# Grouped-query attention of a four-layer block on one Trainium2 core: heads one by one, or in pairs

## What is computed

```python
# third layer (mixer_a): band of radius 128 and a sink per head
s = einsum('bnqhgd,bnkhd->bnhgqk', qb, kw) * HEAD_DIM ** -0.5
s = where(mask, s, -inf)
m = maximum(max(s, -1), sink)
p = exp(s - m);  denom = sum(p, -1) + exp(sink - m)
o = einsum(p, vw) / denom
# fourth layer (mixer_b) and all memory heads: softmax(q k^T * HEAD_DIM ** -0.5) v, no mask, no sink
# (mixer_b: q and k pass an RMS norm with a gain per head first)
x = x + rms_norm(concatenate([tok, mo]) @ w_o[i], g_mix_post[i])
```

## Time and profile before

| | |
|---|---|
| median, lowest, highest of 3 | 1790.45, 1789.71, 1795.37 us |
| profiled execution | 1794.06 us, span 1792.3 us |
| PE busy (matmuls) | 1694.7 us, 95% |
| DVE busy (VectorE) | 1246.4 us, 70% |
| ACT busy (ScalarE) | 964.7 us, 54% |
| mean granted clock of TensorE | 0.976 |
| heads of the third layer, first scores to first tile of the projection | 1194.25 to 1234.79 us |
| heads of the fourth layer, the same | 1515.16 to 1553.18 us |

### The profile page before, as it was taken

One profiled execution on the slowest core, in us unless ns is written; L12 is line 12 of the kernel. 1 busy time (PEld: TensorE's weight loads), 2 busy tenths in 40 slices (PEclk: granted clock), 3 DMA queues, 4 the chain that ended last, 5 costly groups with the idle time before them and its releaser, 6 DMA issues.

```text
span 1792.3 us, 29338 instructions
## 1 busy us (share of the span) xinstructions
PE 1694.7 (95%) x10696; PEld 1502.6 (84%) x10696; DVE 1246.4 (70%) x1826; ACT 964.7 (54%) x1580; POOL 74.9 (4%) x74
## 2 busy tenths in 40 slices
PE   7999999799999999998899999988899978989997
PEld 6999987499999899986689999866799977689996
DVE  6876785357666786676757776767776677667665
ACT  5655563455554655555545654556555554755453
POOL 0100110000000100011201000000000002000000
PEclk9999999899999999999999999999899988989998
DMA  6665454145655465554234656531365534036552
GB/s 226 208 210 185 157 173 152 48 165 192 204 178 188 138 219 194 180 181 132 83 133 150 207 191 193 178 122 51 107 215 191 185 119 141 32 110 215 191 190 73
DMA packets 79331, 287.04 MB, mean 160 GB/s; under 512 B 8848, under 2 KB 9232, under 8 KB 79008
## 3 DMA queue, kind: packets, MB, share of 16 engines
q1 hardware_dynamic: 78336, 282.25, 47.8%
q0 software_dynamic: 608, 3.15, 0.5%
q10 hardware_dynamic: 320, 0.74, 0.1%
HBM read 285.05 MB, written 1.05 MB: 160 GB/s over the span
## 4 chain that ended last, share of the span: by engine, by line
PE 35%; issue 11%; DVE 6%; ACT 3%; DMA 1%; POOL 0%; POOLq 0%; SPq 0%; ACTq 0%; DVEq 0%
PE ps L1805 8%; PE ps L1746 5%; PE ps L1809 4%; PE ps L1791 4%; PE ps L1793 4%; PE ps L1792 4%; PE ps L2131 2%; PE ps L2095 1%; DMA raw<-units 1%; DVE inv L1601 1%; ACT prob L1033 1%; PE ps L1679 1%; DVE wlo L1090 1%; PE ps L2119 1%; DVE x L1323 1%
## 5 line engine op out<-in xcount | busy, mean ns | idle before, releaser
L1254 DVE TENSOR_TENSOR wlo<-raw,whi 128x1024 fp32r<-128x1024 f32 x380 | 463.4, 1223 | 128.1 <-ACT whi L850 126.8
L1805 PE MATMUL ps<-acts,whi 128*128 128x512 f32 x2016 | 506.9, 393 | 1.5 <-DVE prob L1261 0.9
L850 ACT ACTIVATE whi<-raw 128x1024 fp32r<-128x1024 f32 x380 | 398.1, 1051 | 100.1 <-PE ps L1809 70.1
L1805 PEld LDWEIGHTS ps<-acts,whi 128*128 128x128 f32 x2016 | 362.9, 189 | 67.5 <-DVE prob L1261 1.3
L1791 PE MATMUL ps<-hid_hi,wlo 128*128 128x256 f32 x1056 | 298.8, 283 | 0.0
L1792 PE MATMUL ps<-hid_hi,whi 128*128 128x256 f32 x1056 | 298.8, 283 | 0.0
L1793 PE MATMUL ps<-hid_lo,whi 128*128 128x256 f32 x1056 | 298.8, 283 | 0.0
L1809 PEld LDWEIGHTS ps<-acts,wlo 128*128 128x128 f32 x2016 | 275.0, 190 | 19.7
L1809 PE MATMUL ps<-acts,wlo 128*128 128x256 f32 x2016 | 281.1, 282 | 0.0
L1090 DVE TENSOR_TENSOR wlo<-raw,whi 128x1024 fp32r<-128x1024 f32 x154 | 187.4, 1236 | 131.1 <-ACT whi L724 130.5
L724 ACT ACTIVATE whi<-raw 128x1024 fp32r<-128x1024 f32 x154 | 159.6, 1054 | 140.3 <-DMA raw<-units 103.0
(11 more groups left out here) (194 smaller groups left out, 1898.6 us busy)
## 6 DMA issues: line engine op xcount, KB each, us to landing
raw<-units SPq DMA_DIRECT2D x534, 512.0 KB, 4.0
arena<-mem_in POOLq DMA_DIRECT2D x2, 1024.0 KB, 7.1
x<-x_in SPq DMA_DIRECT2D x4, 256.0 KB, 4.7
arena<-mem_in POOLq DMA_DIRECT2D x4, 256.0 KB, 4.9
out<-x SPq DMA_DIRECT2D x4, 256.0 KB, 2.1
const<-const_in ACTq DMA_DIRECT2D x1, 560.0 KB, 5.1
row<-row_in ACTq DMA_DIRECT2D x1, 134.0 KB, 5.7
gain<-gain_in SPq DMA_DIRECT2D x1, 76.5 KB, 1.9
```

Of the source, the lines that this page charges most:

```text
L850: nc.scalar.activation(whi[:, u % RING, :], raw[:, u % RAW, :], ACT.Copy).then_inc(hi_ready, 1)
L1254: V.tensor_tensor(wlo[:, u % RING, :], raw[:, u % RAW, :], whi[:, u % RING, :].bitcast(F32), ALU.subtract).then_inc(lo_ready, 1)
L1805: T.matmul(ps[:, bank, :], whi[:, slot, w], acts[:, k].rearrange("p e s -> p (e s)"), start=k == 0, stop=False)
```

## The change

Both grouped-query layers call a new loop, `pair_attention`, with eight pairs instead of sixteen heads; the linear and the latent layer keep `attention`. The pairs have semaphores of their own. VectorE adds the mask, takes the maximum, scales, adds the sink's share, takes the reciprocal and multiplies once for two heads (the scaled maximum is made in place in `top`). ScalarE copies both heads' transposed probabilities in one instruction from banks 4 and 5, so that `probT` is filled once a pair. TensorE puts the outputs of both heads in one bank, head 0 on partitions 0 to 63 and head 1 on 64 to 127, with the matmuls of the two heads in alternation. VectorE, and no longer ScalarE, writes the high part; it covers both heads with one copy and then one subtraction. The steps also shift: scores of pair `s`, transposes of pair `s`-2 and outputs of pair `s`-3 on TensorE; maximum of `s`, multiplication of `s`-2 and split of `s`-4 on VectorE; exponentials of `s`-1 and copy of `s`-3 on ScalarE.

The core of the diff (new semaphores, `self.done` and the calls of `pair_attention` left out; a semaphore wait that names `base + p + 1` waits for pair `p`):

```diff
# helpers
+        def pair_scores(p):
+            return ps[:, 2 * (p % 2):2 * (p % 2) + 2, :].rearrange("p e (t k) -> p e t k", t=TT)
+        def of_pair(a, p):
+            return a[:, 2 * (p % 2):2 * (p % 2) + 2]
# ScalarE, for s in range(n + 4), n = 8
+                        if 1 <= s <= n:
+                            p = s - 1
+                            act.wait_ge(pair_top, base + p + 1)
+                            if p >= 2:
+                                act.wait_ge(pair_turned, base + p - 1)
+                            for e in range(2):
+                                job, j = jobs[2 * p + e], 2 * (p % 2) + e
...
+                            ins.then_inc(pair_exp, 1)
+                        if 3 <= s < n + 3:
+                            p = s - 3
+                            act.wait_ge(pair_turned, base + p + 1)
+                            if p >= 1:
+                                act.wait_ge(pair_out, base + p)
+                            nc.scalar.activation(probT[:].rearrange("p e k q -> p (e k q)"),
+                                                 ps[:, 4:6, :].rearrange("p e n -> p (e n)"), ACT.Copy
+                                                 ).then_inc(pair_copied, 1)
+                        if s >= n + 4 - AHEAD:
+                            self.split(1)
# VectorE, for s in range(n + 4)
+                        if s < n:
+                            p, job = s, jobs[2 * s]
+                            dve.wait_ge(pair_scored, base + p + 1)
+                            if job["mask"] is not None:
+                                middle = of_pair(ps, p)[:, :, P:3 * P]
+                                self.step(V.tensor_tensor(middle, middle, job["mask"].unsqueeze(1).to_broadcast([P, 2, 2 * P]),
+                                                          ALU.add))
+                            self.step(V.tensor_reduce(of_pair(top, p), pair_scores(p), AX_X, ALU.max))
...
+                            ins.then_inc(pair_top, 1)
+                        if 2 <= s < n + 2:
+                            p, job = s - 2, jobs[2 * s - 4]
+                            dve.wait_ge(pair_exp, base + p + 1)
...
+                            self.step(V.reciprocal(of_pair(inv, p), of_pair(total, p)))
+                            V.tensor_tensor(of_pair(prob, p), of_pair(prob, p),
+                                            of_pair(inv, p).unsqueeze(3).to_broadcast([P, 2, TT, S]), ALU.mult
+                                            ).then_inc(pair_prob, 1)
+                        if s >= n + 4 - AHEAD:
+                            self.split(1)
+                        if s >= 4:
+                            p, kt = s - 4, jobs[2 * s - 8]["kt"]
+                            dve.wait_ge(pair_out, base + p + 1)
+                            o = ps[:, 6 + p % 2, 0:S]
+                            V.tensor_copy(act_hi[:, kt, :], o).then_inc(pair_hi, 1)
+                            dve.wait_ge(pair_hi, base + p + 1)
+                            V.tensor_tensor(act_lo[:, kt, :], o, act_hi[:, kt, :].bitcast(F32), ALU.subtract
+                                            ).then_inc(pair_lo, 1)
# TensorE, for s in range(n + 3)
+                        if s < n:
+                            if s >= 2:
+                                pe.wait_ge(pair_exp, base + s - 1)
+                            for t in range(TT):
+                                for e in range(2):
+                                    job = jobs[2 * s + e]
+                                    ins = T.matmul(pair_scores(s)[:, e, t, :], job["q"][t], job["k"], start=True, stop=True)
+                            ins.then_inc(pair_scored, 1)
+                        if s == n:
+                            pe.wait_ge(pair_exp, base + n)
+                            self.out_tile(0)
+                        if s == n + 1:
+                            self.out_tile(1)
+                        if 2 <= s < n + 2:
+                            p = s - 2
+                            pe.wait_ge(pair_prob, base + p + 1)
+                            if p >= 1:
+                                pe.wait_ge(pair_copied, base + p)
+                            for e in range(2):
...
+                                        ins = T.transpose(ps[:, 4 + e, k * S + t * P:k * S + (t + 1) * P],
+                                                          prob[:, 2 * (p % 2) + e, t, k * P:(k + 1) * P], ident)
+                            ins.then_inc(pair_turned, 1)
+                        if s == n + 2:
+                            self.out_tile(2)
+                        if s >= 3:
+                            p = s - 3
+                            pe.wait_ge(pair_copied, base + p + 1)
+                            if p >= 2:
+                                pe.wait_ge(pair_lo, base + p - 1)
+                            for k in range(TT):
+                                for e in range(2):
+                                    job = jobs[2 * p + e]
+                                    ins = T.matmul(ps[64 * e:64 * e + HD, 6 + p % 2, 0:S], job["v"][k], probT[:, e, k, :],
+                                                   start=k == 0, stop=k == TT - 1)
+                            ins.then_inc(pair_out, 1)
```

More of the change, by code:

```diff
@@ L1017, in gqa, with pair_attention @@
                         self.evacuate(4, vm, LOWER, "mem2")
-                    self.attention(gqa_jobs(b))
+                    self.pair_attention(gqa_jobs(b))
+                def pair_attention(self, jobs):
+                    n, base = len(jobs) // 2, self.pairs
+                    for s in range(n + 4):
+                        if 1 <= s <= n:
[5 more added lines that the diff above has]
+                                job, j = jobs[2 * p + e], 2 * (p % 2) + e
+                                if job["sink"] is not None:
+                                    nc.scalar.activation(es[:, j, :], top[:, j, :], ACT.Exp, bias=job["sink"])
+                                for t in range(TT):
+                                    scale = HD ** -0.5 if job["rms"] is None else query_scale(job)[:, t:t + 1]
+                                    ins = nc.scalar.activation(prob[:, j, t, :], ps[:, j, t * S:(t + 1) * S], ACT.Exp,
+                                                               scale=scale, bias=top[:, j, t:t + 1],
+                                                               accum_out=total[:, j, t:t + 1])
+                            ins.then_inc(pair_exp, 1)
[9 more added lines that the diff above has]
+                            self.split(1)
+                    self.pairs += n
+                pairs = 0
                 def attention(self, jobs, beside={}):
@@ L1584, in gqa, with pair_attention @@
                     self.g += 1 + 3 + 2
-                    self.attention(gqa_jobs(b))
+                    self.pair_attention(gqa_jobs(b))
+                def pair_attention(self, jobs):
+                    n, base = len(jobs) // 2, self.pairs
+                    for s in range(n + 4):
+                        if s < n:
[6 more added lines that the diff above has]
+                            self.step(V.tensor_reduce(of_pair(top, p), pair_scores(p), AX_X, ALU.max))
+                            if job["rms"] is not None:
+                                name, h = job["rms"]
+                                dve.wait_ge(scale_ready, list(QUERY_SCALE).index(name) + 1)
+                                scale = stat(name, means).rearrange("p (t h) -> p h t", t=TT)[:, h:h + 2, :]
+                                ins = V.scalar_tensor_tensor(out=of_pair(top, p), in0=of_pair(top, p), scalar=-1.0,
+                                                             in1=scale, op0=ALU.mult, op1=ALU.mult)
+                            elif job["sink"] is None:
+                                ins = V.tensor_scalar(of_pair(top, p), of_pair(top, p), -HD ** -0.5, None, ALU.mult)
+                            else:
+                                sinks = minus_sink[:, job["head"]:job["head"] + 2].unsqueeze(2).to_broadcast([P, 2, TT])
+                                ins = V.scalar_tensor_tensor(out=of_pair(top, p), in0=of_pair(top, p),
+                                                             scalar=-HD ** -0.5, in1=sinks, op0=ALU.mult, op1=ALU.min)
+                            ins.then_inc(pair_top, 1)
+                        if 2 <= s < n + 2:
+                            p, job = s - 2, jobs[2 * s - 4]
+                            dve.wait_ge(pair_exp, base + p + 1)
+                            if job["sink"] is not None:
+                                self.step(V.tensor_tensor(of_pair(total, p), of_pair(total, p), of_pair(es, p), ALU.add))
+                            if p >= 2:
+                                dve.wait_ge(pair_prob, base + p - 1)
+                            self.step(V.reciprocal(of_pair(inv, p), of_pair(total, p)))
[12 more added lines that the diff above has]
```

(7 more changed lines are left out.)

24 lines of the change are left out of this document (22 added, 2 removed).

## The result

The changed kernel takes 1826.32 us (median of 4, 1824.02 to 1830.83). The kernel before, run beside it, takes 1792.4 (4 executions, 1789.71 to 1795.37). The ratio is 1.0192, 95% interval 1.0164 to 1.022: slower by 33.9 us. The profiled execution took 1824.02 us.

A forecast was written before the change was run, and what follows sets the result against it. VectorE was taken to bound the third layer's heads, with TensorE nearly full in the fourth's; +15 us for the loop and +21 for the clock, carried to the median of 1790.45, gave 1826, range 1802 to 1842.

The forecast's parts named there:

- The order on the queues: Both layers' heads: TensorE and VectorE take turns, with a 3 to 4 us wait for the multiplication at every turn.
- Rival (d): Both layers' heads: the loop does not bind and the shorter VectorE sums set the pace, 1776 us; chance 0.05.
- The length of the loop: One round of TensorE and VectorE per pair: 7.18 us masked, 6.27 unmasked, with eight turns at about 1.2.
- The tails behind the heads: Behind each layer's heads: two turns of eight instead of four add 1.2 us.
- The sum for the loop: Both layers at the full clock: +8.4 us in the third and +6.6 in the fourth, together +15.0.
- The clock: TensorE's holes lower the granted clock in both layers: 11 blocks of turn, outputs and scores at 1.9 us, +21.
- Rival (a'): Both layers: every block of turn, outputs and scores at the low clock throughout, +15 and +31, 1836 us; chance 0.15.
- Rival (b): Both layers: the loop as worked out, but the clock holds, +15, 1805 us; chance 0.16.
- Column groups: TensorE's outputs of two heads run side by side on two column groups: 1.05 us a pair, otherwise 2.1.
- Rival (c): Both layers: the loop, and the two column groups do not overlap, about 1843 us; chance 0.10.
- VectorE's sum: VectorE's work per pair: 4.63 us instead of 5.50 masked, 3.72 unmasked.
- The merged multiplication: On VectorE, one product of 1024 columns saves nothing: 1.22 us against 1.24 for four of 256.

The follow-up runs named there:

- e1_swap: The changed kernel with VectorE's addition, reciprocal and multiplication of pair s-2 placed before the mask, maximum and scaling of pair s: 1787.55 us.
- e3_fill: The changed kernel with 5 (unmasked 4) unread filler matmuls on TensorE between the scores of a pair and the next turn, from the third pair on: 1805.56 us.
- e9_all: e7_copy_first with the high copy given back to ScalarE, behind the exponentials, one for both heads: 1782.62 us.
- e8_one_group: e4_serial with both heads' outputs on the same column group, partitions 0 to 63, so head 1's outputs are missing from their place: 1842.54 us.
- e7_copy_first: e1_swap with ScalarE's copy of pair s-3 placed before the exponentials of pair s-1: 1784.06 us.
- e5_four: The changed kernel with the merged multiplication of 1024 columns replaced by four products of 256 columns by a scalar per partition: 1828.03 us.
- e4_serial: The changed kernel with the output matmuls issued head by head instead of alternating between the two heads: 1828.44 us.

## Why the prediction was right

1826 was predicted and 1826.3 measured. The steps, one by one.

*The order on the queues.* That TensorE and VectorE take turns was read from the order of the lines, and it holds: 12 waits at the turn, 3.60 to 3.81 us in the third layer. In the fourth they are 2.88, just under the 3 to 4 that I named. Scores of neighbouring pairs are 8.8 to 9.4 us apart in the steady part of the third layer and 6.1 to 8.8 in the fourth, as forecast. e1_swap shows the cause by removing it. Rival (d) fell with it.

*The length of the loop.* e3_fill has it at the full clock: 6.97 us a masked pair (1213.02 to 1220.00, and on to 1226.97), 7.18 predicted; 6.05 unmasked (1545.02 to 1551.07), 6.27 predicted. Nearly the whole difference is one term: eight turns take 1.02 us from start to start, and I had 1.2, nearly twice the 0.64 of four in the earlier trace rows. The tails behind the heads, for which I took the same 1.2, cost 0.9.

*The sum for the loop.* +15 was predicted, 11.2 is what e3_fill leaves. The loop's shorter period accounts for 5 x 0.2 in each layer and the tails for 0.6. That leaves 1.2, and one more thing is worth 1.7: the fourth layer's first scores took 3.68 us at the low clock before, and I carried that into the forecast. In the changed kernel and in e3_fill they take 2.00, 1.7 less. In e9_all they take 3.73 again, so it isn't a property of one order. The 0.5 us between the two stay unexplained.

*The clock.* +21 was predicted as 11 blocks of 1.9, and e3_fill puts it at 20.8 by the medians. That holes this long bring the clock down is shown. The 1.9 is partly luck: it was a choice between 1.4 and 2.8 that one low stretch supported, and the loss is spread otherwise than I had it. Turns and outputs run mostly at 1.2 GHz (3.81 us in the window with clock 0.50, against 2.04 in e3_fill), which is 1.8 a block. Scores vary from 1.13 to 2.08. And 1.7 us are in the third layer's first tile, which I hadn't priced. Rival (a') would have had every block low from end to end, scores too. The scores at 1217.13 took 1.13 us, and the block at 1572.88 was at the full clock altogether, so it was too strict. Rival (b), a clock that holds, fell. e3_fill's 1805.6 is the case it priced at 1805, but the nearness is chance: the loop was 4 us shorter than in that price, and the kernel before stood 4 us higher (1794.64). The Trainium skill, TensorE: Matmul & The Clock Gate, in the section on HAM oscillation, has the clock fall anew at each burst that follows a wait. The trace agrees for nearly all turns and outputs (clock 0.54 and 0.50 in the windows above), and not for the block at 1572.88 nor for the scores, which end the burst.

*Column groups.* Side by side, as the earlier trace rows suggested: eight records in 1.08 us, one head's time in the earlier trace rows. Rival (c) is what e8_one_group builds. I priced it at 1843, and it came to 1842.5. But only 9.5 of its 14 us are in the stretches that the price was about, so the nearness is partly luck.

*VectorE's sum.* 4.63 was predicted for a masked pair and 4.40 measured in e7_copy_first without a hole, since instructions follow each other somewhat closer than I had them. Unmasked 3.72 was predicted; e7_copy_first's pairs of 3.5 us bound it from above. The gain of the merge is thus real, and the changed kernel hides all of it behind the loop. The merged multiplication alone is worth nothing, as predicted, and e5_four confirms it. That the rows agree with a faster product by a scalar, as the prediction has it, was read too freely: 1.24 against 1.22 us is no difference, and in e5_four it is 1.05 against 1.14.

*The closeness of the total.* The loop was 4 us too dear (15 against 11.2). The median of before that I started from, 1790.45, came out 2 us higher beside the changed kernel (1792.4). The rest of the program was 1.9 us shorter in the profile. And the profiled executions lie 29.9 us apart, the medians 33.9: the one of before was 1.7 above its median, that of the changed kernel 2.3 below. The four cancel. The mechanism and the size of the two terms are shown; agreement to a microsecond is chance.

*What I missed.* That a second loop, between TensorE and ScalarE, lay under the first, 2.5 us a pair shorter in the third layer and 1.5 in the fourth. I had named ScalarE only as emptier. It doesn't bear on the changed kernel, but it holds back more than a third of the gain from whoever mends only the first: e1_swap is 7.1 us below the kernel before, e7_copy_first 11.5, each against the executions beside it.

## What to carry to other kernels

When the distance of a software pipeline changes, follow one item around the queues of two engines: what stands ahead of it on each, and what that waits for. If the circle closes within one step and is longer than any engine's own work, its length is the new period, however much the merge has saved on either engine. Before giving up such a merge, exchange the two blocks on the waiting engine so that the ready work stands first, then look for the next circle behind it. And price TensorE's holes twice, once as idle time and once for the clock that they cost the work behind them; here the second was the larger, 21 us against 11 (about 14 at an equal clock).

## What was unexpected of the hardware

Matmuls of two column groups ran side by side even when they were issued one group after the other (e4_serial: starts in twos 13 ns apart, eight records in 1.09 us). I had expected a loss of 10 us or more. That the two of a start belong to two heads is inferred from e8_one_group, where no two start together. How far apart the two may stand in the queue before that ends, no run here shows; in this kernel two matmuls of the other group lay between.

Useless matmuls of 2.0 to 2.4 us a pair made the kernel 21 us faster (e3_fill). Holes of 1.45 us once in 7 us left the granted clock at 1.00; in the changed kernel it was 0.50 right behind every hole of 2.88, 3.60 and 3.81 us but one.
